# Long convolution with two pairs of banks for forming, filter samples on four 64x64 tiles, sums by accumulating transfers, and a last projection on eight banks

## What is computed

```python
x0, x1, v = jnp.split(short_conv_centred(hy_in, conv_w, conv_b), 3, axis=-1)
k = hyena_filter(L, ...)            # (2 L, 1024)
y_a = x0 * long_conv_bidir(v * x1, k, hyena_skip) * jax.nn.silu(hy_gate)
y = jnp.concatenate([y_a, y_b], axis=-1) @ w_out
x = x + rms_norm(y, post_norm_w)
```

```python
h = h @ w_o                         # h: (2048, 64), w_o: (64, 2 * 1024)
h_fwd, h_bwd = h[:, :D_A] * decay, h[:, D_A:] * decay
l1 = sum(abs(h_fwd), axis=0) + sum(abs(h_bwd[1:]), axis=0)
k = concatenate([h_fwd, zeros((1, D_A)), h_bwd[1:][::-1]], axis=0) / (l1 + EPS)
U, K = rfft(u, n=2 * L), rfft(k)    # along the sequence
y = irfft(U * K, n=2 * L)[:L] + u * skip
```

## Time and profile before

| | |
|---|---|
| median of 3 runs | 3100.89 us (3099.92 to 3102.55) |
| profiled execution | 3099.8 us, span 3098.0 us |
| mean granted TensorE clock | 0.989 of full |
| PE busy | 2977.7 us (96%) |
| DVE busy | 2477.7 us (80%) |
| ACT busy | 870.9 us (28%) |
| POOL busy | 381.8 us (12%) |
| long convolution | from 2221.5 us to about 2746 us |
| last projection | from about 2746 us to the end |

### The profile page before, as it was taken

One profiled execution on the slowest core, in us unless ns is written; L12 is line 12 of the kernel. 1 busy time (PEld: TensorE's weight loads), 2 busy tenths in 40 slices (PEclk: granted clock), 3 DMA queues, 4 the chain that ended last, 5 costly groups with the idle time before them and its releaser, 6 DMA issues. The chain is left out here.

```text
span 3098.0 us, 33135 instructions
## 1 busy us (share of the span) xinstructions
PE 2977.7 (96%) x12866; PEld 2161.9 (70%) x12866; DVE 2477.7 (80%) x2746; ACT 870.9 (28%) x1449; POOL 381.8 (12%) x512
## 2 busy tenths in 40 slices
PE   8999999999998999999999999999899999889999
PEld 4444444656776888888888888887656666678887
DVE  7979999898996888999899999998478979862221
ACT  3000000596334331111121211112444735731111
POOL 2212121001343441011000000000000100000000
PEclk9999999999999999999999999999999999999999
DMA  7576553301447547777666566652322331454231
GB/s 217 171 178 166 170 148 90 116 1 59 143 157 243 173 134 193 196 194 185 172 168 160 149 177 163 160 157 70 113 92 82 111 122 41 150 180 124 84 109 41
DMA packets 218869, 430.53 MB, mean 139 GB/s; under 512 B 21872, under 2 KB 135192, under 8 KB 210840
## 3 DMA queue, kind: packets, MB, share of 16 engines
q1 hardware_dynamic: 189256, 324.58, 34.9%
q0 software_dynamic: 28304, 95.44, 12.4%
q10 hardware_dynamic: 1152, 8.39, 0.7%
HBM read 324.53 MB, written 85.98 MB: 133 GB/s over the span
## 5 line engine op out<-in xcount | busy, mean ns | idle before, releaser
L1898 PE MATMUL PS<-HX,WH 128*128 128x512 f32 x1536 | 599.2, 390 | 6.9 <-DVE MB L1780 5.0
L1899 PE MATMUL PS<-HX,WH 128*128 128x512 f32 x1536 | 598.3, 390 | 0.0
L1900 PE MATMUL PS<-HX,WL 128*128 128x512 f32 x1536 | 598.2, 389 | 0.0
L849 PE MATMUL PS<-M 128*128 128x512 f32 x1088 | 472.2, 596 | 8.1 <-DVE M L650 6.8
L849 PEld LDWEIGHTS PS<-M 128*128 128x128 f32 x1088 | 207.3, 191 | 272.8 <-issue 263.5
L1898 PEld LDWEIGHTS PS<-HX,WH 128*128 128x128 f32 x1536 | 288.9, 188 | 67.9 <-DVE MB L1780 5.9
L120 DVE SCALAR_TENSOR_TENSOR HP<-MF,HP 128x1024 f32<-128x1024 f32 x252 | 323.5, 1284 | 14.1 <-DMA MF<-h_scratch 5.9
L1900 PEld LDWEIGHTS PS<-HX,WL 128*128 128x128 f32 x1536 | 288.7, 188 | 60.1
L1899 PEld LDWEIGHTS PS<-HX,WH 128*128 128x128 f32 x1536 | 288.8, 188 | 59.7
L120 DVE SCALAR_TENSOR_TENSOR M<-M 128x1024 f32<-128x1024 f32 x160 | 205.6, 1285 | 27.4 <-DMA M<-c_feat 21.8
L2591 PE MATMUL PS<-WH,YH 128*128 128x512 f32 x512 | 202.1, 395 | 9.3 <-DVE HP L2730 5.2
(11 more groups left out here) (230 smaller groups left out, 5085.9 us busy)
## 6 DMA issues: line engine op xcount, KB each, us to landing
MF<-h_scratch SPq DMA_DIRECT2D x380, 256.0 KB, 5.1
M<-c_feat POOLq DMA_DIRECT2D x186, 256.0 KB, 4.3
MF<-w_in SPq DMA_DIRECT2D x52, 512.0 KB, 4.5
WL<-MF POOLq DMA_DIRECT2D x46, 512.0 KB, 4.5
M<-u_scratch SPq DMA_DIRECT2D x16, 1024.0 KB, 4.9
M<-c_decay POOLq DMA_DIRECT2D x48, 256.0 KB, 2.9
M<-x SPq DMA_DIRECT2D x18, 512.0 KB, 4.2
M<-w_in SPq DMA_DIRECT2D x18, 512.0 KB, 5.3
```

What stands on the lines that cost most here:

```text
L849: ins = t.matmul(ps[:, c, :], wt[:, k], HT[:, k, TC * c:TC * c + TC], start=(k == 0), stop=(k == KD - 1))
L1898: t.matmul(dst, wh, hh, start=(k == 0), stop=False)
L1899: t.matmul(dst, wh, hl, start=False, stop=False)
L1900: ins = t.matmul(dst, wl, hh, start=False, stop=(k == KD - 1))
```

## The change

- `forms` uses banks 0, 1 and 2, 3 in turn, two pairs instead of three; from the third bin of a chunk it waits until the products of the bin two before are made, instead of three before.
- The inverses alternate between banks 4 and 5 (before: bank 6 alone).
- `generate` puts the two halves of a sample set in two banks: in the second, forward and backward half change places, so that the four matmuls of 64 x 64 use the four tiles of the array. The first 16 sets alternate between banks 4, 5 and 6, 7; the later ones use 6, 7. The table `c_tneg` is rolled to match.
- `filter_first` has two matmuls of 256 columns per group in place of one of 512, one with `AF` and one with `AF_SWAPPED` (a new constant, rows rolled by 64), each reading and writing every second column.
- The absolute values of chunks 1 to 3 are added into `KSUM` by an accumulating transfer from POOL's queue, each after the one before has landed, in place of DVE's L2241. The first chunk stays with DVE.
- In `output` four tiles of two banks take turns, so tile `i` waits for `scaled` of tile `i - 4`, and in the joint part tile 1 runs three rows behind tile 0.

Left out of the diff are the names of new semaphores and regions, the wait for one more constant, and three more places where `i % 2` became `i % 4`.

```diff
@@ -1983,13 +1984,20 @@
             return 4 * n + 4 + n // 16 + 1
 
         def banks_of(n):
-            return 2 * (n % 16 % 3), 2 * (n % 16 % 3) + 1
+            return 2 * (n % 2), 2 * (n % 2) + 1
 
         def lag_of(cc):
             return 2 if cc == NCH - 1 else 1
 
-        def sample_bank(kq):
-            return 6 + kq % 2 if kq < 16 else 7
+        def sample_place(kq):
+            bank = 4 if kq < 16 and kq % 2 else 6
+            return PS[:, bank:bank + 2, 0:CH]
+
+        def inverse_bank(n):
+            return 4 + n % 2
+
+        def sums_before(kq):
+            return 15 * (kq // 16 - 1) + kq % 16 - 1
 
         const2_in = sem("c3b_in")
         fc_in = sem("fc_in")
...
@@ -2113,9 +2122,20 @@
 
         @block.gpsimd
         def _(g):
+            def absolute_added(kq):
+                if kq < 16 or kq % 16 == 0:
+                    return
+                g.wait_ge(kabs_done, kq + 1)
+                if sums_before(kq):
+                    g.wait_ge(kabs_summed, 16 * sums_before(kq))
+                g.dma_start(KSUM, KABS[kq % 2], accum_op=ALU.add).then_inc(kabs_summed, 16)
+
             for kq in range(16, 16 * NCH):
                 g.wait_ge(k_weighted, kq - 3)
                 g.dma_start(DEC[kq % 4], A["c_decay"][kq - 16]).then_inc(decay_in[kq % 4], 16)
+                absolute_added(kq - 4)
+            for kq in range(16 * NCH - 4, 16 * NCH):
+                absolute_added(kq)
 
         @block.scalar
         def _(s):
...
@@ -2137,8 +2157,14 @@
                         s.wait_ge(l1_done, cc)
                     s.activation(KSUM, out, ACT.Abs).then_inc(kabs_done, 1)
                 else:
-                    if 15 * cc + j > 2:
-                        s.wait_ge(kabs_added, 15 * cc + max(j - 2, 0))
+                    if cc == 0 and j > 2:
+                        s.wait_ge(kabs_added, j - 2)
+                    elif cc and j <= 2:
+                        s.wait_ge(kabs_added, 15)
+                        if cc > 1:
+                            s.wait_ge(kabs_summed, 16 * 15 * (cc - 1))
+                    elif cc:
+                        s.wait_ge(kabs_summed, 16 * (sums_before(kq) - 1))
                     s.activation(KABS[j % 2], out, ACT.Abs).then_inc(kabs_done, 1)
 
             def inputs_out(ug):
...
@@ -2159,14 +2185,14 @@
 
             def inverse_out(n):
                 s.wait_ge(inv_done, n + 1)
-                s.activation(UTB[:, n % 16], PS[:, 6, :].rearrange("p (y c) -> p y c", y=2), ACT.Copy).then_inc(z_done, 1)
+                s.activation(UTB[:, n % 16], PS[:, inverse_bank(n), :].rearrange("p (y c) -> p y c", y=2), ACT.Copy).then_inc(z_done, 1)
 
             decays(0)
             for kq in range(16):
                 if kq < 15:
                     decays(kq + 1)
                 absolute(kq)
-            s.wait_ge(const2_in, 16 * 5)
+            s.wait_ge(const2_in, 16 * 6)
             inputs_out(0)
             inputs_out(1)
             for cc in range(NCH):
...
@@ -2229,15 +2255,15 @@
                 if j == 0 and cc >= 2:
                     v.wait_ge(ia_done, 8 * (cc - 1))
                 out = KB[cc % 2][:, 512 * j:512 * j + 512]
-                v.tensor_tensor(out.rearrange("p (c x) -> p x c", x=2), PS[:, sample_bank(kq), :].rearrange("p (x c) -> p x c", x=2),
+                v.tensor_tensor(out.rearrange("p (c x) -> p x c", x=2), sample_place(kq),
                                 DEC[kq % 4].rearrange("p (x c) -> p x c", x=2), ALU.mult).then_inc(k_weighted, 1)
 
             def summed(kq):
-                cc, j = kq // 16, kq % 16
+                j = kq
                 if j:
                     v.wait_ge(kabs_done, kq + 1)
                     if j > 1:
-                        v.wait_ge(kabs_added, 15 * cc + j - 1)
+                        v.wait_ge(kabs_added, j - 1)
                     v.tensor_tensor(KSUM, KSUM, KABS[j % 2], ALU.add).then_inc(kabs_added, 1)
 
             def filter_turned(cc, groups):
...
@@ -2343,11 +2367,7 @@
                         weights_low(v, kept, L, n)
                     continue
                 if cc + 1 < NCH:
-                    filter_turned(cc + 1, range(0, 1))
-                    summed(16 * cc + 30)
-                    filter_turned(cc + 1, range(1, 2))
-                    summed(16 * cc + 31)
-                    filter_turned(cc + 1, range(2, 6))
+                    filter_turned(cc + 1, range(0, 6))
                     outputs_turned(2 * cc, (0,))
                     filter_turned(cc + 1, range(6, 11))
                     outputs_turned(2 * cc, (1,))
...
@@ -2386,8 +2406,8 @@
                 for x in range(2):
                     for d in range(2):
                         p = slice(HID * d, HID * d + HID)
-                        ins = t.matmul(PS[p, sample_bank(kq), CH * x:CH * x + CH], h3[p, 2 * j + x], WOC[cc % 2][p],
-                                       start=True, stop=True)
+                        to = HID * (d if x == 0 else 1 - d)
+                        ins = t.matmul(sample_place(kq)[to:to + HID, x], h3[p, 2 * j + x], WOC[cc % 2][p], start=True, stop=True)
                 ins.then_inc(kgen_done, 1)
 
             def filter_first(cc):
...
@@ -2398,9 +2418,15 @@
                     n = 16 * cc + g
                     if g >= 4:
                         t.wait_ge(kt_done, n - 3)
-                    t.matmul(PS[:, n % 4, :], AF, KTC[cc % 2][:, 16 * g:16 * g + 16], start=True, stop=True).then_inc(ak_done, 1)
+                    formed = PS[:, n % 4, :].rearrange("p (c a y) -> p c a y", a=16, y=2)
+                    for y, forward in enumerate((AF, AF_SWAPPED)):
+                        ins = t.matmul(formed[:, :, :, y], forward, KTC[cc % 2][:, 16 * g:16 * g + 16, :, y], start=True, stop=True)
+                    ins.then_inc(ak_done, 1)
                 ksum = KSUM.rearrange("p (c x) -> p x c", x=2)
-                t.wait_ge(kabs_added, 15 * cc + 15)
+                if cc:
+                    t.wait_ge(kabs_summed, 16 * 15 * cc)
+                else:
+                    t.wait_ge(kabs_added, 15)
                 if cc:
                     t.wait_ge(z_done, 16 * cc)
                 if not cc:
...
@@ -2439,14 +2465,14 @@
             def inverse(n):
                 bp = n % 16
                 t.wait_ge(y_done, n + 1)
-                if n:
-                    t.wait_ge(z_done, n)
-                if bp == 0:
-                    t.wait_ge(l1_read, n // 8 + 2)
-                    if n:
-                        t.wait_ge(yc_done, n // 2)
+                if n >= 2:
+                    t.wait_ge(z_done, n - 1)
+                if bp < 2:
+                    t.wait_ge(l1_read, n // 16 * 2 + 2)
+                    if n >= 16:
+                        t.wait_ge(yc_done, n // 16 * 8)
                 for x in range(2):
-                    ins = t.matmul(PS[:, 6, CH * x:CH * x + CH], INV[:, 2 * bp + x], UTB[:, bp, x],
+                    ins = t.matmul(PS[:, inverse_bank(n), CH * x:CH * x + CH], INV[:, 2 * bp + x], UTB[:, bp, x],
                                    start=True, stop=True)
                 ins.then_inc(inv_done, 1)
 
...
@@ -2456,10 +2482,8 @@
 
                 def forms(p):
                     n = 16 * cc + p
-                    if p >= 3:
-                        t.wait_ge(pm_done, n - 2)
-                    if p == 2 and cc:
-                        t.wait_ge(yc_done, 8 * cc)
+                    if p >= 2:
+                        t.wait_ge(pm_done, n - 1)
                     for src, bank, formed in ((KTB[cc % 2], banks_of(n)[0], kf_done), (UTB, banks_of(n)[1], uf_done)):
                         for x in range(2):
                             ins = t.matmul(PS[:, bank, CH * x:CH * x + CH], STRIP[:, 2 * p + x], src[:, p, x], start=True, stop=True)
...
@@ -2531,6 +2555,7 @@
 
 
 W_EARLY = 6
+ROWS_BEHIND = 3
 W_AT = ([2048 * n for n in range(10)] + [25600 + 2048 * n for n in range(4)] + [38912, None])
 YH_AT, YL_AT = (34816, 36864), (21504, 23552)
 
...
@@ -2587,7 +2612,7 @@
     at = place_of(i, W_ORDER[n])
     yh, yl = L.YH[i % 2][:, at], L.YL[i % 2][:, at]
     wh, wl = (w[n][:, TC * half:TC * half + TC] for w in (L.WH, L.WL))
-    dst = PS[:, 2 * (i % 2) + half, :]
+    dst = PS[:, 2 * (i % 4) + half, :]
     t.matmul(dst, yh, wh, start=(n == 0), stop=False)
     t.matmul(dst, yl, wh, start=False, stop=False)
     return t.matmul(dst, yh, wl, start=False, stop=(n == KY - 1))
...
@@ -2735,16 +2760,23 @@
 
         @block.tensor
         def _(t):
-            for n in range(W_EARLY - 1, KY - 1):
-                first_products(t, kept, L, PS, n)
-            t.wait_ge(wl_done, KY)
-            for i in range(2):
+            def row(i, n):
+                t.wait_ge(wl_done, n + 1)
+                t.wait_ge(yl_done, 2 * (n // KD) + i + 1)
                 for half in range(2):
-                    ins = product(t, L, PS, i, KY - 1, half)
-                ins.then_inc(mm_done, 1)
```

(26 more changed lines are left out.)

## The result

The changed kernel takes 3188.12 us, median of four runs (3185.8 to 3192.68), against 3101.36 us for the kernel before (3099.92 to 3102.55, four runs): 1.0278 times as long, 95% interval 1.0257 to 1.0298. The forecast was 3128 us, 3117 to 3142. The direction was right; the loss is three times the forecast one, 87 us instead of 27. Ratios leave out two executions of the kernel with the projection alone (3699.87 and 4736.35 us, at mean granted clocks of 0.773 and 0.593), since they were far slower than the rest.

The account below looks back on a forecast made before the run. It took TensorE, VectorE and the second stage's dependency loop to be balanced. Terms 15.9 + 14.7 - 1.1 - 1.2 - 0.8 = +27.5 us on 3100.89 gave 3128 us, range 3117 to 3142.

Parts of the forecast that it names:

- Step 5: First transform in two 256-column matmuls: slightly longer on TensorE, fewer adds on VectorE, together -1.1 us.
- rival C: First transform: strided output or input doubles its time, +56 us, 3184 us; chance 4%.
- Step 1: Second stage, first three chunks: forming on two bank pairs waits longer and holds up the inverse; +15.9 us.
- the ring: Second-stage loop from a bin's products through inverse and copies to products two bins later: 7.94 us before, 8.73 forecast.
- Step 2: Last chunk's second stage: the same forming wait, 8.21 us for two bins; +14.7 us.
- rival D: Second stage: pauses bring TensorE's clock down more than before, +20 us, 3148 us; chance 3%.
- Step 3: Filter samples on four tiles: four matmuls in 0.6 us instead of 1.06, worth nothing.
- Step 4: Absolute values added by transfers: a sum takes 3.5 us, hidden with 0.8 to spare; worth nothing in the stage.
- Rival B: Second stage: sums landing in over 4.3 us set the pace, +10.5 us, 3139 us; chance 12%.
- Steps 6 and 7: The ends: inverses on two banks at the last chunk's end, -1.2 us; then the reordered last projection, -0.8 us.
- Rival A: Second stage: the new forming wait is hidden and bins get faster, -9 us, about 3089 us; chance 7%.

Follow-up runs that it names:

- the projection alone: Kernel before with only the last projection on eight banks and tile 1 three rows behind tile 0: 3100.71 us, ratio 0.9993.
- the ladder: Kernel before with the first transform replaced by matmuls on constants, reading words 8, 16, 32, 64 and 128 bytes apart: 3139.72 us.
- two-pairs kernel: Kernel before with only forming on two pairs of banks instead of three: 3144.77 us, ratio 1.0137.
- the kernel with the inverse ahead: Changed kernel with TensorE making the inverse ahead of the next forming in each second-stage turn: 3147.81 us, ratio 1.0154.
- filled kernel: Kernel before with two pairs of banks, plus thrown-away matmuls ahead of odd bins' forming in the last chunk: 3139.37 us, ratio 1.0117.
- the split transform: Kernel before with only the first transform split in two 256-column matmuls, every second column read and written: 3148.89 us, ratio 1.0155.
- the repaired kernel: Changed kernel with first-transform reads 8 bytes apart, written densely, and the inverse ahead of the next forming: 3104.42 us, ratio 1.0009.

## Why the prediction was right in sign and wrong in size

**Step 5, the first transform, is the one that failed.** The prediction wrote -1.1 and named "nothing, or twice the time" as bounds. It came out at twice the time: +12.35 us before the first chunk and +37.6 between chunks, +50 in all. The upper bound was right, but it went into rival C and not into the range. Of the 58.5 us by which the span's growth exceeds the forecast sum, 51.1 lie in this step's stretches, 8.9 in the last chunk and 1.3 in the first three; the ends give back 2.8. The row that was to speak against it, "an input with a stride (L2465 reads every second word) runs at full pace", was true of another distance: L2465's words are 8 bytes apart, those of the new transform 2 KB. The ladder puts the step between 8 and 16 bytes. It was rival C, priced at +56 and given 4%, and it did not replace the main case but came on top of it. The rivals had been written as alternatives where two of them could be true together.

A rule was at hand that the prediction didn't weigh. The Trainium skill (Advanced Engine Details and Errata, Memory Cachelines) says that SBUF is read in lines of 16 bytes and that two hits on a line are needed for full performance; 8 bytes apart gives two hits, 16 bytes one, and the ladder agrees (0.93 us a group at 8 bytes, 1.72 to 1.85 from 16 on). The same section says that any non-contiguous pattern in PSUM slows matmuls down significantly; the variant with strided writes does not agree, 15.8 us for 64 pieces as with dense ones.

**Step 1, the ring in three chunks, was right:** 8.72 us for two bins against 8.73, its inner times within 0.02, and +17.3 us against +15.9. The two-pairs kernel shows it by itself, and the kernel with the inverse ahead shows that the queueing behind the wait, not the number of banks as such, makes the loss.

**Step 2, the last chunk, had the ring right and put the clock at nothing:** +23.6 against +14.7. The filled kernel separates the two parts: +15.4 is the ring, with the forecast 8.21 us for two bins, and 6 us of the two-pairs kernel's 21.4 are the clock. In the changed kernel, where no filled variant ran, the excess over the forecast is 8.9. The prediction had rival D, the clock falling in the pauses, at 3% and argued from the one pause of 2.65 us in the earlier trace rows after which the pace was full. A single pause is no evidence on one that comes back every two bins, and in the changed kernel pauses of nearly one length end either way: after 2.33 us eight pieces took 2.08 us, after 2.49 us 3.57.

**Step 3, the four tiles:** 0.66 us for four matmuls in the ring, 0.6 taken, and worth nothing, as said. TensorE waited 56.0 us on L2347 in the four chunks. In the first 16 sample sets, ahead of the first chunk, the gain was not even there. The window from 2230 to 2245 us, in the kernel before and in the changed one:

```profile
2230.00:2245.00 15.00, 11.33 (x80) 6.80 (x80) 12.74 (x21) 13.80 (x32) 1.12 (x2) 1.00 0.68 273
```

```profile
2230.00:2245.00 15.00, 10.36 (x72) 3.10 (x72) 12.86 (x22) 13.54 (x30) 1.67 (x3) 0.50 0.75 291
```

The granted clock was 1.00 before and 0.50 after, and a set took 1.15 us on four tiles where it took 1.13 on two. From 2235 to 2245 us it is 0.50 in all five kernels here with the four tiles and 1.00 in all nine without; no run changes the tiles alone.

**Step 4, the sums by transfers, were hidden:** landings of 3.3 us against 3.5, no wait of ScalarE on them, and with the sums back on VectorE the same time. Rival B did not come. The Trainium skill (DMA: Bandwidth & Descriptors, anatomy of a DMA on the GpSimd path) gives an estimate of 2.6 us; an adding transfer of 256 KB within SBUF took 3.3. The 0.1 us for POOL's wake-up stands in no row: where a transfer waits for the one before, issues follow every 3.8 us, 0.5 above the landing. So the cover was thinner than said, about 0.6 us and not 0.8; with the ring at 7.64 us, POOL waits 88.4 us for landings.

**Steps 6 and 7, the ends,** gave -4.8 together against -2.0, inside their bounds, but step 6 not by its reason. It held that later waits are shorter, so that less work would run at half pace. The last inverse still ran at half pace, after a longer wait, 3.98 us where before had 1.02:

```profile
2799.90 2.07 PE L2475 MATMUL PS<-M 128*128 128x256 f32 x4 [3.98 <-DVE M L2349]
```

Of the -4.8, 3.2 lie ahead of row 8 of the projection (47.08 us after the last first product, 50.32 before), and 1.5 behind it. The 1.5 agrees with the projection alone, where the wait for VectorE turned into one for the weights; -0.8 was forecast. The 3.2 cannot be credited to the change: the split transform and the two pairs of banks, which leave the end alone, were 2.6 and 2.8 us shorter from the last first product to the end.

One sum of the prediction is off: the upper bounds of steps 3, 6 and 7 add up to +5.4, not +4.2, which changes nothing here.

**Rival A did not come:** forming started at 2.15 us in the ring, where it had to start before 0.95.

Still open is why the clock falls after some pauses and not after others of the same length, and why the repaired kernel's runs spread over 18 us (the fastest at a mean clock of 0.984, the slowest at 0.978). The kernel before spread over 5 us beside it, and over 21 in a later set of seventeen runs.

## What to carry to other kernels

Split a matmul's moving operand so that each piece still reads words at most 8 bytes apart, or pairs; the order in which the words are taken is free if the next engine can put it back. Before taking away a buffer, look at what stands behind the new wait in the engine's list: putting the inverse ahead of the forming gave back 40 us with the same banks. Then look at what the new order makes TensorE wait for, and at its granted clock behind that wait. And when a row is cited against a rival, check that it has the rival's numbers, distance and repetition, and give rivals that can be true together a joint case.

## What the runs showed of the hardware

A 256-column f32 matmul piece takes 0.23 us when its moving words are 8 bytes apart or in pairs, and 0.43 to 0.46 from 16 bytes to 2 KB, without a further step. Writing every second word into PSUM cost nothing that shows: 15.8 us for 64 pieces, as with dense writes.

TensorE's granted clock, 0.99 in the last chunk before, had a mean of 0.83 with pauses of 2.49 us every two bins, and 1.00 when useless matmuls filled part of the pauses: eight pieces took 3.57 us after a pause and 1.97 without. Not every such pause brings it down (2.08 us for eight pieces after 2.33). It can also fall behind the stage, as in the two-pairs kernel, where 64 pieces of 64 columns took 13.76 us, and did not in the filled kernel, 7.65. Late in the first 16 sample sets it was 0.50 with four tiles and 1.00 with two, and a set took 1.15 and 1.13 us.

Adding transfers of 256 KB within SBUF, from POOL's queue, landed in 3.3 us, and one waiting for the other they followed every 3.8.
